# The first part of a hybrid block: score pieces regrouped behind products, two searches for one, one counting block for ScalarE

## The reference, cut to what matters

```
a = rms_norm(x, g_mix) @ w_in                    # 2048 x 2520, split in 14 pieces
rel   = relu(q_idx . k_idx)                      # 8 index heads, 64 wide
score = sum over heads of w_idx * rel            # for each query and key
score = where(key <= query, score, -inf)
sel   = top 256 of each query's scores           # block of 128 queries by block
```

## Time and profile before

| what | us |
|---|---|
| time, median of 3 runs | 2831.49 (2829.45 to 2832.87) |
| profiled execution, span | 2830.9 (no other time of this execution is listed) |
| PE busy | 2596.2 (92%) |
| VectorE busy | 1813.7 (64%) |
| ScalarE busy | 1283.1 (45%) |
| GpSimd busy | 922.8 (33%) |
| mean granted TensorE clock | 0.965 of full speed |

### The profile page before, as it was taken

The page is one execution under the profiler, slowest core; times in us unless marked ns, Lnnn a source line. Parts: engine busy times, 40 slices in busy tenths (PEclk is TensorE's granted clock), DMA queues, the critical chain, the costliest instruction groups (busy, mean ns, idle before and its releaser), DMA issues. The chain is left out here.

```text
span 2830.9 us, 34992 instructions
## 1 busy us (share of the span) xinstructions
PE 2596.2 (92%) x10908; PEld 1642.9 (58%) x10909; DVE 1813.7 (64%) x2566; ACT 1283.1 (45%) x2400; POOL 922.8 (33%) x925
## 2 busy tenths in 40 slices
PE   6988779999987899898799979999999999998998
PEld 3634323344863445444688756666666666665787
DVE  2176999699977788876333486644644444743676
ACT  2277867967956676766321222222222222222322
POOL 2377877700011111121000043434444444433221
PEclk9999989999997899999899989999999999999999
DMA  5101131113152123222544459975776665973663
GB/s 151 63 33 42 32 58 38 35 63 98 38 169 78 62 73 102 76 71 74 200 143 143 177 224 356 351 273 210 282 270 227 237 223 201 347 286 138 198 216 132
DMA packets 221474, 438.08 MB, mean 155 GB/s; under 512 B 22888, under 2 KB 91048, under 8 KB 221224
## 3 DMA queue, kind: packets, MB, share of 16 engines
q1 hardware_dynamic: 199400, 357.78, 36.8%
q0 software_dynamic: 13312, 47.32, 5.3%
q10 hardware_dynamic: 8640, 31.46, 2.7%
HBM read 331.14 MB, written 105.38 MB: 154 GB/s over the span
## 5 line engine op out<-in xcount | busy, mean ns | idle before, releaser
L2504 DVE CAST p_high<-p_low 128x2048 fp32r<-128x2048 f32 x128 | 203.0, 1586 | 400.4 <-PE p_psG L2611 293.3
L698 PE MATMUL p_psP<-home,p_ring 128*128 128x512 f32 x832 | 366.3, 598 | 0.0
L2627 PE MATMUL p_psY<-p_wd,p_hT 128*128 x752 | 330.9, 593 | 2.4 <-ACT p_hT L2686 2.2
L2506 DVE TENSOR_TENSOR p_low<-p_low,p_high 128x2048 fp32r<-128x2048 f32 x128 | 318.9, 2492 | 4.4
L698 PEld LDWEIGHTS p_psP<-home,p_ring 128*128 128x128 f32 x832 | 157.3, 191 | 205.0 <-issue 204.9
L2627 PEld LDWEIGHTS p_psY<-p_wd,p_hT 128*128 128x128 f32 x752 | 139.3, 190 | 160.6 <-issue 160.4
L727 PE MATMUL p_psI<-p_kI,p_qI 64*128 64x512 f32 (+3 forms) x608 | 148.1, 596 | 62.9 <-ACT p_relu L589 62.8
L2547 POOL TENSOR_TENSOR p_xT_low<-p_xT,p_xT_high 128x512 fp32r<-128x512 f32 x94 | 186.1, 1998 | 3.4 <-ACT p_xT L2671 3.4
L2609 PE MATMUL p_psG<-p_high,p_xT_high 128*128 128x512 f32 x376 | 167.2, 445 | 15.8 <-DVE p_low L2506 8.2
L2553 POOL TENSOR_TENSOR p_hid<-p_act_g,p_act_u 128x512 f32<-128x512 f32 x47 | 62.2, 1324 | 307.7 <-ACT p_act_u L2681 294.8
L603 ACT ACTIVATE p_relu<-p_relu,p_small 128x512 f32<-128x512 f32 (+3 forms) x266 | 161.5, 662 | 0.0
(11 more groups left out here) (423 smaller groups left out, 5833.4 us busy)
## 6 DMA issues: line engine op xcount, KB each, us to landing
p_low<-in_w_expert_gate_dram SPq DMA_DIRECT2D x32, 2048.0 KB, 13.5
p_low<-in_w_expert_up_dram SPq DMA_DIRECT2D x32, 2048.0 KB, 18.3
p_wd<-in_w_expert_down_dram SPq DMA_DIRECT2D x32, 2048.0 KB, 10.7
y_dram<-p_y ACTq DMA_DIRECT2D x47, 512.0 KB, 8.1
p_xt<-in_x_dram SPq DMA_DIRECT2D x32, 512.0 KB, 4.7
y_dram<-p_clear SPq DMA_DIRECT2D x32, 512.0 KB, 4.3
proj_f<-p_stage SPq DMA_DIRECT2D x52, 256.0 KB, 2.4
p_ot<-o_dram SPq DMA_DIRECT2D x16, 512.0 KB, 4.5
```

Source lines behind the costliest of these rows:

```text
L698: mm = pe.matmul(psP[0:n, i % 2, :], w, aT[:, k, c * CH:(c + 1) * CH], start=k == 0, stop=k == KD - 1)
L2504: dve.tensor_copy(high[:, m, k, :], low[:, par, m, k, :].bitcast(F32)).then_inc(high_done, 1)
L2506: dve.tensor_tensor(low[:, par, m, k, :], low[:, par, m, k, :].bitcast(F32), high[:, m, k, :].bitcast(F32), ALU.subtract).then_inc(w_split, 1)
L2627: mm = pe.matmul(psY[:, c, :], hT[:, k, :], wd[:, bass.ds(at, 1), k, c * CH:(c + 1) * CH].rearrange("p a f -> p (a f)"), start=k == 0, sto ...
```

## The change

`GROUPS` gets five groups, (4, 5, 6, 7) being split into (4, 5) and (6, 7). `HELPED` says how many blocks of a group ScalarE counts: one (block 11) in the group of 8 to 11, two in the last. `order` has the first f behind the first four x tiles. Two pieces stand behind each product of chunk 1 from its first on, which places blocks 2 and 3 behind four wide products; from there on two behind a narrow product and behind one of chunk 1, four behind the others. The last four x tiles are turned just before the first narrow product of chunk 2. VectorE scales and copies these tiles between its first and second search. GpSimd adds blocks 2 and 3 before it fills the bias rows, and issues the loads of blocks 4's and 5's queries behind them. `deal()` follows with its assumed times (`SEARCH_AT` is 100, eleven us for the late tiles).

```diff
-GROUPS = [(2, 3), (4, 5, 6, 7), (8, 9, 10, 11), (12, 13, 14, 15)]
+GROUPS = [(2, 3), (4, 5), (6, 7), (8, 9, 10, 11), (12, 13, 14, 15)]
-HELP_FROM = (-1, -1, 15, 30)
-SEARCH_AT, LEAN, COUNT = 155.0, 0.3, 0.18
+HELP_FROM = (-1, -1, -1, 15, 30)
+HELPED = (0, 0, 0, 1, 2)
+SEARCH_AT, LEAN, COUNT = 100.0, 0.3, 0.18
+LAST_X = 12
...
-        order = [("Q", 0), ("Q", 1), ("X", 0), ("X", 1), first(0, 0), first(1, 0), ("Q", 2), first(2, 0), first(3, 0), first(4, 0), ("X", 2)]
-        order += [narrow(t) for t in range(4)] + [("Q", 3), first(0, 1), first(1, 1), ("X", 3)] + [first(m, 1) for m in (2, 3, 4)]
+        order = [("Q", 0), ("Q", 1), ("X", 0), first(0, 0), ("X", 1), first(1, 0), ("Q", 2), first(2, 0), first(3, 0), first(4, 0), ("X", 2)]
+        order += [narrow(t) for t in range(4)] + [("Q", 3)]
         done = 0
-        for t in range(4, 8):
-            order += [narrow(t)] + [("R", done + i) for i in range(2)]
-            done += 2
-        for i in range(place["f", 0, 2], len(products)):
-
+        for i in range(place["f", 0, 1], len(products)):
+            if i == place[512, 2 * TPC]:
+                order += [("X", 3)]
             there = [j for j in SCORED if place[512, j // TPC * TPC + TPC - 1] + 1 <= i]
-            upto = min(first_rel[there[-1], IP - 1] + len(chunks(there[-1])), done + 5)
+            upto = min(first_rel[there[-1], IP - 1] + len(chunks(there[-1])), done + (2 if products[i][0] == "t" or products[i][2] == 1 else 4))
             order += [("M", i)] + [("R", r) for r in range(done, upto)]
             done = upto
...
             weigh_ready(0)
             load_qI(2)
             load_qI(3)
+            for t in range(LAST_X, NT):
+                inverse_root(t)
+            for j in (2, 3):
+                scored(j)
+            load_qI(4)
+            load_qI(5)
 
             pool.memset(rows_a[:, :], 0.0).then_inc(filled, 1)
...
                 act.wait_ge(flipped, g * (NBITS + 1) + NBITS - b)
-                act.wait_ge(sensed, 2 * k)
-                for c in range(2):
-                    j = GROUPS[g][2 + c]
+                act.wait_ge(sensed, sensed_by[g, b])
+                own = len(GROUPS[g]) - HELPED[g]
+                for c in range(HELPED[g]):
+                    j = GROUPS[g][own + c]
...
-                    own = 2 if (g, b) in turns else n
+                    own = n - HELPED[g] if (g, b) in sensed_by else n
...
             for g in range(len(GROUPS)):
+                if g == 1:
+                    turned_over(LAST_X, NT)
                 search(g)
```

More of the change, by code:

```diff
@@ L267, in project_and_select @@
         helped = [(g, b) for g in SHARED for b in range(HELP_FROM[g], -2, -1)]
-        turns = {which: i for i, which in enumerate(w for w in helped if w[1] >= 0)}
+        sensed_by, n = {}, 0
+        for g, b in helped:
+            if b >= 0:
+                sensed_by[g, b] = n
+                n += HELPED[g]
         LATE = [j for g in SHARED for j in GROUPS[g]]
@@ L274, in deal @@
             next_pe, act_at, pool_at, dve_at = 0, 25.0, 0.0, SEARCH_AT
-            masked, flips, counted, out = {}, {}, {}, []
+            masked, flips, counted, late_x, out = {}, {}, {}, [], []
             steps = [(g, b) for g in range(len(GROUPS)) for b in range(NBITS, -2, -1)]
@@ L301, in on_dve @@
                     js = GROUPS[g]
+                    if (g, b) == (1, NBITS) and not late_x:
+                        late_x.append(True)
+                        dve_at += 11.0
                     if b == NBITS:
@@ L340, in deal @@
                     assert b >= 0 or all(kind != "R" for kind, _ in order[k:])
-                    act_at = max(act_at, ready) + 0.4 + sum((0.28 + 0.0008 * width(j)) for j in GROUPS[g][2 if b >= 0 else 0:])
+                    act_at = max(act_at, ready) + 0.4 + sum((0.28 + 0.0008 * width(j)) for j in GROUPS[g][len(GROUPS[g]) - HELPED[g] if b >= 0 else 0:])
                     counted[g, b] = act_at + 0.1
@@ L486, in _ @@
             pool.dma_start(mask_dram[1, :, 0:2 * P], hidden_first[:, :]).then_inc(mask_stored, 16)
-            for t in range(8, NT):
+            for t in range(8, LAST_X):
                 inverse_root(t)
@@ L517, in add, with scored @@
                 pool.tensor_tensor(dst, dst, relu[:, n % NRELU, 1, 0:c1 - c0], ALU.add).then_inc(summed, 1)
+            def scored(j):
+                for i in range(IP):
+                    for ci in range(len(chunks(j))):
+                        add(j, i, ci)
+                if 4 <= j and j + 2 < NT:
+                    load_qI(j + 2)
+                pool.wait_ge(summed, first_rel[j, IP - 1] + len(chunks(j)))
+                diag = scores_of(S_low, S_high, j)[:, width(j) - P:width(j)]
+                pool.tensor_tensor(diag, tri_big[:, :], diag, ALU.add).then_inc(S_masked, 1)
             weigh_ready(0)
@@ L532, in _ @@
                 pool.tensor_copy(rows_s[:, at], raw_s[:, b:b + 1].broadcast_to([SH, n])).then_inc(filled, 1)
-            for j in SCORED:
+            for j in SCORED[2:]:
                 if j % TPC == 0:
                     weigh_ready(j // TPC)
[L536 to L543, removed]
+                scored(j)
             for b in range(2):
@@ L786, in _, with turned_over @@
             dve.wait_ge(gain_loaded, 16)
[L787 to L791, removed]
+            def turned_over(t0, t1):
+                scale(t0)
+                for t in range(t0, t1):
+                    if t + 1 < t1:
+                        scale(t + 1)
+                    copy_x(t)
+            turned_over(0, LAST_X)
             def count(jj, j, value):
@@ L833, in settle @@
             def settle(g):
-                v = flip[:, 2:4]
-                side, up, low, high, carried, change = (ints[:, i, :] for i in range(6))
-                for jj in (2, 3):
+                own, n = len(GROUPS[g]) - HELPED[g], len(GROUPS[g])
+                v = flip[:, own:n]
+                side, up, low, high, carried, change = (ints[:, i, 0:HELPED[g]] for i in range(6))
+                for jj in range(own, n):
                     W = width(GROUPS[g][jj])
@@ L859, in settle @@
                 chain(dve.tensor_tensor(change, high, up, ALU.bitwise_xor))
-                at = chain(dve.tensor_scalar(side, cnt[:, 2:4], float(TOPK), -1.0, ALU.is_ge, ALU.mult))
+                at = chain(dve.tensor_scalar(side, cnt[:, own:n], float(TOPK), -1.0, ALU.is_ge, ALU.mult))
                 dve.wait_ge(step, at)
```

9 lines of the change are left out of this document (4 added, 5 removed).

## The result

| | before | after |
|---|---|---|
| median, us | 2832.18 (2829.45 to 2833.69, 10 runs) | 2838.45 (2837.42 to 2840.73, 10 runs) |
| ratio to before, 95% interval | | 1.0025 [1.0017, 1.0034] |
| span of the profiled execution | 2830.9 | 2835.8 |
| first part over (ScalarE's first row behind it) | 845.0 | 852.7 |
| the rest | 1985.9 | 1983.1 |

The kernel after is slower by 0.25%, some 6 us, beyond noise; the forecast was 2829.5, no change. The trace puts the loss in the first part: +7.7 us, against a forecast of -1.4. The rest, untouched, is 2.8 us shorter in this execution. From here on "before" and "after" also stand for the two kernels, "the part" for the first part and "run n" for experiment n; "the hold" is the wait of ScalarE's stage copy (L586 now) for an older store, and "helped bits" are the third group's last 16.

The account below looks back on a forecast made before the run. VectorE's search was taken to bound the first part. Third group's start -3.8, its last 16 bits +9.1 and settling -1.7 gave +3.6; less 5.0 at the end, -1.4, rounded to -2: 2829.5 us, range 2808 to 2846.

Parts of the forecast that it names:

- the hold: Before the third group: ScalarE's stage copy waits 24 us for a store behind the bias rows; block 11 masked at 412.
- helped bits: Third group's last 16 bits, VectorE counting three blocks and ScalarE one: 96 us, against 86.9 before.
- the first f now fills that hole: Start: the first wide product fills PE's 10.8 us idle; chunk 2's first product at about 134, VectorE starting at 122.5.
- 5.0 us go: End of the part: no copies between ScalarE's last sign and the p products, saving 5.0 us.
- 64 us after the issue: ScalarE's stage copy: its wait ends 64 us after the bias rows' store is issued, from 299.5 to 364.5.
- the hold does not bind: Rival, third group's start: block 11 masked before 388, so all 24 us stay: 2805, chance 0.12.
- the late turning misses: Rival, late x tiles: waits there delay bias store and block 11; VectorE at 200, not 189: +11, 2840, chance 0.09.
- one sign a slot: Rival, third group's last 16 bits: ScalarE full, 28 us more, 2858, or 2843 with half the slots; chance 0.14.
- The split and VectorE's arrival: Blocks 4 to 7 as two groups: 16 us more small steps, 188 us; VectorE at the third group at 387.6.
- Settling and the fourth group: After the third group's bits: settling counts one block, not two, -1.7 us; the fourth group's 193.7 us stay.

Follow-up runs that it names:

- Experiment 1: Kernel after, but VectorE copies x tile 3 before it scales tile 4: 2831.53 us, ratio 0.9999 to the kernel before.
- run 3: Kernel after, with twenty unused 512-column products on PE in front of the first p product: 2837.03 us, ratio 1.0017 to the kernel before.
- run 4: Kernel after, with the first product back behind the second turning of x: 2838.02 us, ratio 1.0021 to the kernel before.
- run 6: Kernel after, with up to five pieces behind a wide product instead of four: 2845.72 us, ratio 1.0049 to the kernel before.
- run 7: Kernel after, with ScalarE counting two blocks (10 and 11) in the third group instead of one: 2865.38 us, ratio 1.0117 to the kernel before.
- run 8: Kernel after, with blocks 4 to 7 searched as one group again: 2854.83 us, ratio 1.0083 to the kernel before.
- run 12: Kernel after, with x tile 3 copied first and the late turning of tiles 12 to 15 undone, store on SP's queue: 2833.2 us, ratio 1.0003.
- run 2: Kernel after, with the bias rows' store issued earlier and from ScalarE's queue instead of SP's: 2825.12 us, ratio 0.9978 to the kernel before.
- run 9: Kernel after, with x tile 3 copied before tile 4's scaling and the bias rows stored from ScalarE's queue: 2817.1 us, ratio 0.9949.
- run 10: Kernel before, with only the bias rows' store issued from ScalarE's queue: 2836.0 us, ratio 1.0017 to the kernel before.
- run 11: Kernel after, with x tile 3 copied first, bias rows stored from ScalarE's queue and the late turning of tiles 12 to 15 undone: 2827.55 us, ratio 0.9982.

## Why the prediction was wrong, step by step

- **The step that failed: "the first f now fills that hole".** The forecast put the first product at 17.7; it ran at 29.27. It used the timeline of PE and left out VectorE's order, in which a scaling that waits for tile 4 stands ahead of the copy that the product reads. The earlier trace rows name the releaser of PE's hole: DVE home L783, a copy. The question not asked was what that copy stood behind. The low clock behind the hole, 8.87 us for the product, was not in the forecast either. So chunk 2's first product came at 143.1, not at 134, VectorE's start at 132.6, not at 122.5, block 11's mask at 417.4, not at 412. Experiment 1 removes only this and the third group starts at 410.7, the part ends at 844.9 (forecast 843.4). None of the signs that the forecast named for being wrong came: the third group did not start before 400, the helped bits stayed between 86 and 104, and PE's last narrow product ended near 800, before the signs. What it had named as showing it right was a first search count near 122, and there the error is plain: 132.6.
- **A term that was missing.** "5.0 us go" at the end was right (818.57 to 818.66 has no gap), but before the change PE had work nearly up to the p products: it was busy for 17.3 us of 795 to 814, at a granted clock of 1.00. In after it was busy for 5.5 us of the same stretch, at 0.74. 2.8 us come back in the first eight p products (run 3). It could be seen: the forecast itself has PE's products end 20 us and more before the signs.
- **The hold.** Its mechanism was right. The wait was 29.0 us instead of 24, since the products in front of it were ready earlier against the store. The forecast's "64 us after the issue" is the best number of the working: the copy begins 63.6 us after the second issue in the trace before, in after, and in runs 1, 3, 4, 6, 7, 8 and 12, to within 0.03. The rival "the hold does not bind" did not come. Its 2805 priced an absent hold at 24 us; run 2, which takes the hold away, gains 13.3 and stays at 2825, and with the start mended too (run 9) the time is 2817.
- **The rival "the late turning misses".** This one came nearest, 2840 for 2838.45. It had VectorE reach the late tiles at 200 instead of 189, and VectorE reached them at 198.1. But the turning itself did not miss (PE came at 199.0 and waited 3.4 us in all); VectorE was late from the start. The forecast put the chance at 0.09, since it took VectorE's start as bounded within 5 us, and it was 10 off.
- **Helped bits.** Forecast 96, measured 96.9; ScalarE is busy 89.4 of 97 us, where the forecast had 91 of 96. Ten of the 16 bits take 5.0 us and six 7.2 to 8.9; the waits for signs sum to 16.7 us, where the forecast had 14.5 (96 less 81.5). The rival "one sign a slot" needed 104 or more and did not come.
- **The split and VectorE's arrival.** Forecast 387.6 at the third group, measured 400.9 (418.03 less the wait). 7.5 of the 13.3 us are there when the second group starts (206.99 for 199.5), which is what the late start leaves; 5.9 are in the two searches of the split group (193.9 for 188). Of these, 4.3 stand in the choosing for blocks 6 and 7: 18.7 us (382.2 to 400.9), and 14.4 before (401.4 to 415.8). The forecast counted only the small steps. All 13.3 us are hidden by the wait for block 11, until the hold goes.
- **Settling and the fourth group.** -1.3 us (forecast -1.7) and -0.6 us (forecast 0).

Summed on VectorE: +2.3 at the third group, +10.0 helped bits, -1.3 settling, -0.6 fourth group, together 10.4, where the last row is 10.5 later; ScalarE's last sign is 10.0 later, 5.0 go, 2.8 come back: +7.8, as the part's +7.7. Of the 9.1 us between that and the forecast's -1.4, the third group's start is 6.1 (418.0 for 412; experiment 1 gives 7.3 back there) and the clock 2.8. Of the smaller misses, 1.0 too much in the helped bits and 0.6 too little in the fourth group offset each other in part.

## What to carry to other kernels

Before a product is put into a hole, follow the operand it reads through the order of the engine that makes it: what stands in front of that copy, and what does it wait for? Where a change moves the bound to another engine, look for holds that nobody waited for at that place before (a store queued behind a long one), and price them at the place where they now end. In these traces TensorE, left without work for 18.1 us before a short critical run, paid up to 3.1 us for it in that run; and an issue moved to a computing engine has to fall where that engine waits anyway.

## What was not expected of the hardware

- *A long store on a few engines.* The hold ends 63.6 us after the second issue in nine traces, whatever stands before it; the wait itself is between 14.4 and 29.0 us. In after, the DMA engines' mean share is 0.41 from 303 to 345 and 0.27 from 345 to 367, which is 6.6 and 4.3 of 16 engines. The Trainium skill, "DMA: Bandwidth & Descriptors", section "Issuing engines are not separate DMA queues", says that transfers from all engines run on the same 16 DMA engines and interleave, and that another issuer saves only issue time. The runs differ in part: issued from ScalarE's queue, the bias rows still delay SP's stores (72 KB stores land 17.4 us after issue by the median, 1.6 in the kernel after in the same stretch of 190 to 300 us; one copy waits 11.2), but nothing waits 29 us. That agrees with interleaving. But the 13.3 us of run 2 are no saved issue time; they come from the other queue, or from the issue 100 us earlier, which no run separates.
- *The issue blocks its engine.* The issue of the 1536 KB store takes 8.1 us from ScalarE, which stands still for 7.2 of them (run 10). On SP it takes 8.4 us, and SP here only issues transfers.
- *The clock.* After 18.1 us of waiting, the first eight products take 6.47, 6.76, 6.41, 6.40, 6.46, 6.60 and once 5.18 us (after, runs 2, 4, 9, 11, 12 and 1), after 13.6 us of waiting 6.57 (run 6), and after 41.0 us 5.27 (run 7), against 3.70 with PE kept busy.
